# A four-layer token network on one core: norms by token, own waits, the ends, and the experts' down sums

## The chip, the core and the metric

The kernel runs on one core of a Trainium2 chip. The metric is device time in microseconds (us) of one execution; lower is better. A profiled execution gives a trace beside it. The engines are TensorE (PE, with its weight loads PEld), VectorE (DVE), ScalarE (ACT), GpSimd (POOL) and SyncE (SP, which issues most transfers).

## The reference

256 tokens of width 1024 pass a first block (two layers) and a second (two layers), all float32. The part that matters here:

```python
def _rmsnorm(x, g):
    xf = x.astype(jnp.float32)
    y = xf * lax.rsqrt(jnp.mean(xf * xf, axis=-1, keepdims=True) + EPS)
    return (y * g.astype(jnp.float32)).astype(x.dtype)
def adaln(x, g, shift, scale):
    return rmsnorm(x, g) * (1 + scale) + shift
# first block: x += mixer(rmsnorm(x)) @ w_out ; x += conv_ffn(rmsnorm(x)), twice
# second block, with a context of 256 more tokens in its first layer:
# x += mod * mixer(adaln(x)) @ w_out ; x += mod * (swiglu, then 8 experts)(adaln(x)); rmsnorm at the end
    for e in range(N_EXPERTS):
        ye = combine[:, e:e + 1] * swiglu(t, w1[e], w3[e], w2[e]).astype(jnp.float32)
```

The mixers are latent attention beside retention, gated linear attention, and window attention beside a matrix LSTM. Each token takes two of the eight experts.

## The kernel before

The residual `res` lies turned: the 1024 features are 8 tiles of 128 partitions, the 256 tokens (or 2 x 256 with the context) lie along the free axis. Each large product is made of three fast matmuls (`mm3`): a weight chunk is split into a rounded part (`weights_hi`, ScalarE, L1598) and a rest (`weights_lo`, VectorE, L2140), and so is the activation `h` (`h_rounded` on ScalarE, L1616; `h_rest` on GpSimd, L1384). Each engine runs its own program, written out by hand, and meets the others by semaphores. Weights come as 474 chunks, mostly of 1 MB, on SP's queue into a ring of 6 slots; three rounded chunks fit in `ring_hi`. `hi_upto` and `lo_upto` say how far the splits go before the next step of that engine.

There are nine norms with this layout, named in `NORM`: `even`, `ffn0`, `odd`, `ffn1`, `n1_0`, `n2_0`, `n1_1`, `n2_1`, `final`; `n1_0`, `n2_0` and `n1_1` take 512 tokens. In each, ScalarE squares two tiles at a time (`squares`, L1510), TensorE sums over the partitions with a 128x128 of ones, so that every partition gets each token's sum (`sum_squares`, L469; a column per token), ScalarE takes the root of all of it (`root`, L1536), VectorE the reciprocal and then the products with `res` and the gains (`norm`, L2110; L2124 in one instruction per tile, or L2120 for four tiles and L2122 per tile where there is a shift). `h` parts go on to ScalarE, GpSimd and TensorE tile by tile. `keep_warm` (L496) issues matmuls whose result nobody reads.

A `Lane` (L171) counts an engine's own instructions. `step` and `tell` wait for the instruction just issued before anything else is issued; `go` and `send` don't, and `settle` and `sent` wait later. `free` (L1464) marks a PSUM bank free, waits for it, and then raises a named flag; `leave` only marks the bank.

At the start SP loads the constants (with ones and eps among them), x, the columns and the rows of small parameters, then the chunks. VectorE computes the rotary angles, waits for ScalarE's sine, Silu, Exp and Ln, and works out the retention's decay rates in 16 small steps before it splits the chunks of the third projection.

An expert has 22 chunks for its up product and 11 for its down product (`down`, L1276): each of these held two rows of tiles by all 1024 columns, and both halves of 512 columns (PSUM banks 2 and 3) grew together. At the end of an expert ScalarE and VectorE take the two halves out (`expert_out`, L2045 and L2901), and `scatter` (L1217) adds the rows back to the tokens, during the next expert's up product. After the last expert that stands at the end: scatter, residual sums, norm `final`, four stores.

## Time and profile before

| | |
|---|---|
| median of 3 runs | 2541.44 us (2541.11 to 2541.6) |
| profiled execution | 2544.85 us |
| its span, first to last instruction | 2543.1 us |
| granted TensorE clock, mean | 0.97 of full |
| busy: PE, PEld | 2411.4 us (95%), 1996.7 us (79%) |
| busy: DVE, ACT, POOL | 1743.1 us (69%), 1243.2 us (49%), 523.2 us (21%) |
| moved from memory | 500.33 MB, 197 GB/s over the span |

The span is what the trace covers; 1.75 us of the profiled execution's time lie around it. Busy shares are means over stages with very different limits: what an edit is worth has to be read where it stands. The chain of waits is the chain of work that ended last, each step followed back to what released it; an entry there gives start, duration, engine and line. A releaser with a q behind its name is that engine's instruction queue. Matmul durations overlap each other, so a matmul's pitch is smaller than its duration.

### The profile page before, as it was taken

What the parts mean: (1) busy time and instruction counts of PE and PEld (TensorE: products, weight loads), DVE (VectorE), ACT (ScalarE), POOL (GpSimd) and SP (SyncE); (2) the same over time, 40 slices, a digit from 0 to 9 for tenths busy, and PEclk for the clock granted to TensorE, in tenths of its full rate; (3) what the DMA queues carried; (4) which work ended last, traced back from release to release, by engine and by line L of the source; (5) the groups of instructions that cost most, each with busy time, mean ns of one, the idle gap of its engine ahead of it and who ended that gap; (6) DMA issues with size and microseconds to landing.
All of it is one profiled execution on the core that took longest, in us unless ns stands there. A gap on an engine that the chain in (4) does not pass through costs nothing.

```text
span 2543.1 us, 35114 instructions
## 1 busy us (share of the span) xinstructions
PE 2411.4 (95%) x13296; PEld 1996.7 (79%) x13296; DVE 1743.1 (69%) x1895; ACT 1243.2 (49%) x1465; POOL 523.2 (21%) x407
## 2 busy tenths in 40 slices
PE   7999999999999999879999979979999999999997
PEld 5668998868997866658888867578888888888886
DVE  6556874567865766468645357657888888888886
ACT  5444444544433455332222134536777777777774
POOL 1003541004522000031003520003132132232231
PEclk9999999999999998889999989988999999999999
DMA  5574553414552310125555323026989989989894
GB/s 200 194 277 148 185 184 125 176 50 150 183 199 79 116 42 1 48 86 199 200 194 186 131 75 116 10 85 249 359 333 357 353 334 364 345 341 370 333 362 184
DMA packets 71461, 503.64 MB, mean 198 GB/s; under 512 B 8192, under 2 KB 8704, under 8 KB 11264
## 3 DMA queue, kind: packets, MB, share of 16 engines
q1 hardware_dynamic: 70128, 496.75, 53.4%
q0 software_dynamic: 1168, 4.66, 0.5%
q8 instruction: 107, 1.75, 0.3%
q14 instruction: 58, 0.48, 0.1%
HBM read 500.33 MB, written 1.05 MB: 197 GB/s over the span
## 4 chain that ended last, share of the span: by engine, by line
PE 86%; DVE 9%; ACT 3%; issue 1%; POOL 1%; DMA 0%; DVEq 0%; ACTq 0%; SPq 0%; PEldq 0%
PE ps L459 82%; DVE ring_r L2144 1%; PE ps L499 1%; DVE h L2122 1%; POOL h_r L1389 1%; DVE h L2120 1%; DVE areaA L2114 1%; PE ps L1214 1%; DVE h L2124 1%; PE ps L751 1%; DVE areaB L2638 1%; PE ps L602 0%; DVE temp L2207 0%; ACT ring_hi L1506 0%; ACT h L1553 0%
## 5 line engine op out<-in xcount | busy, mean ns | idle before, releaser
L1506 ACT ACTIVATE ring_hi<-ring 128x2048 fp32r<-128x2048 f32 x427 | 808.3, 1893 | 556.6 <-PE ps L459 333.3
L2898 DVE TENSOR_TENSOR ring_r<-ring,ring_hi 128x2048 fp32r<-128x2048 f32 x264 | 619.5, 2349 | 120.3 <-ACT ring_hi L1506 117.6
L459 PE MATMUL ps<-ring_hi,extra_r 128*128 128x512 f32 (+2 forms) x1808 | 612.2, 395 | 31.9 <-DVE ring_r L2144 18.1
L2144 DVE TENSOR_TENSOR ring_r<-ring,ring_hi 128x2048 fp32r<-128x2048 f32 (+3 forms) x163 | 384.3, 2358 | 190.9 <-ACT ring_hi L1506 176.4
L459 PE MATMUL ps<-extra_r,ring_hi 128*128 128x256 f32 (+1 forms) x1432 | 462.1, 323 | 22.3 <-POOL h_r L1389 20.8
L459 PE MATMUL ps<-extra_r,ring_r 128*128 128x256 f32 (+1 forms) x1432 | 457.1, 319 | 0.0
L459 PE MATMUL ps<-h_r,ring_hi 128*128 128x256 f32 (+2 forms) x1400 | 445.0, 318 | 0.0
L459 PEld LDWEIGHTS ps<-ring_hi,extra_r 128*128 128x128 f32 x1808 | 343.4, 190 | 107.1 <-DVE ring_r L2144 21.1
L459 PE MATMUL ps<-ring_r,extra_r 128*128 128x512 f32 (+2 forms) x1104 | 426.2, 386 | 0.0
L459 PEld LDWEIGHTS ps<-extra_r,ring_hi 128*128 128x128 f32 x1432 | 273.2, 191 | 46.5 <-POOL h_r L1389 24.1
L459 PEld LDWEIGHTS ps<-extra_r,ring_r 128*128 128x128 f32 x1432 | 273.2, 191 | 19.1
L459 PEld LDWEIGHTS ps<-h_r,ring_hi 128*128 128x128 f32 (+1 forms) x1400 | 267.2, 191 | 17.6
L459 PEld LDWEIGHTS ps<-ring_r,extra_r 128*128 128x128 f32 x1104 | 211.2, 191 | 38.7 <-issue 0.2
L1449 POOL TENSOR_TENSOR areaA_r<-areaA,cst 128x256 fp32r<-128x256 f32 x88 | 120.3, 1367 | 576.5 <-ACT areaA L2036 576.5
L459 PE MATMUL ps<-ring_hi,h_r 128*128 128x512 f32 (+2 forms) x400 | 150.3, 376 | 0.0
L1389 POOL TENSOR_TENSOR h_r<-h,extra_r 128x256 fp32r<-128x256 f32 x80 | 83.5, 1058 | 281.5 <-ACT extra_r L1506 281.4
L459 PE MATMUL ps<-ring_hi,areaB_r 128*128 128x512 f32 x352 | 139.8, 397 | 0.0
L459 PE MATMUL ps<-areaA_r,ring_hi 128*128 128x256 f32 (+1 forms) x736 | 139.5, 288 | 0.0
L459 PE MATMUL ps<-ring_r,areaA_r 128*128 128x512 f32 x352 | 138.0, 392 | 0.0
L459 PE MATMUL ps<-ring_hi,areaA_r 128*128 128x512 f32 x352 | 137.7, 391 | 0.0
L459 PEld LDWEIGHTS ps<-areaA_r,ring_hi 128*128 128x128 f32 x736 | 115.9, 192 | 1.3
L1409 POOL TENSOR_TENSOR areaA_r<-areaB,areaA_r 128x256 fp32r<-128x256 f32 x44 | 115.7, 2630 | 3.5
(356 smaller groups left out, 3123.2 us busy)
## 6 DMA issues: line engine op xcount, KB each, us to landing
ring<-in_experts SPq DMA_DIRECT2D x264, 1024.0 KB, 4.9
ring<-in_stream SPq DMA_DIRECT2D x202, 1024.0 KB, 4.9
ring<-in_stream SPq DMA_DIRECT2D x6, 512.0 KB, 3.6
ring<-in_stream SPq DMA_DIRECT2D x2, 576.0 KB, 3.6
res<-in_xT SPq DMA_DIRECT2D x1, 1024.0 KB, 5.7
res<-in_ctxT POOLq DMA_DIRECT2D x1, 1024.0 KB, 8.2
h<-in_consts POOLq DMA_DIRECT2D x2, 512.0 KB, 4.9
areaB<-in_cond_rows POOLq DMA_DIRECT2D x1, 1024.0 KB, 7.5
```

Of the source, the lines that this page charges most:

```text
L459: return pe.matmul(o, l, r, start=start, stop=stop, skip_group_check=True)
L499: pe.matmul(ps[:, u.bank, :], warm_l, warm_r, start=True, stop=True, skip_group_check=True)
L751: m = pe.transpose(ps[:, u.bank, k * P:(k + 1) * P], pair_p[:, 2 * (n % 2) + hd, k * P:(k + 1) * P], ident)
L1214: m = pe.transpose(ps[:, 3, s * P:(s + 1) * P], mprod[:, n % 2, s * P:(s + 1) * P], ident)
L1389: pool.tensor_tensor(h_lo[:, hf, k, :], h[:, hf, k, :], h_hi[:, hf, k, :].bitcast(F32), ALU.subtract).then_inc(sig("h_lo"), 1)
L1409: pool.tensor_tensor(lo, src, hi.bitcast(F32), ALU.subtract).then_inc(sig("hidden_ready"), 1)
L1449: pool.tensor_tensor(hi, mturn[:, n % 2, :], ones[:, 0:1].broadcast_to([P, NM]), ALU.mult).then_inc(sig("moe_hi"), 1)
L1506: return act.activation(dst, src, ACT.Copy)
L2114: S(dve.reciprocal(rs, rs))
L2120: S(TTN(h[:, hf, k:k + 4, :], res[:, hf, k:k + 4, :], bc(rs[:, hf * T:(hf + 1) * T], 1, [P, 4, T]), ALU.mult))
L2144: L.tell(TTN(ring_lo[:, s, 0:n], ring[:, s, 0:n], ring_hi[:, j % HIS, 0:n].bitcast(F32), ALU.subtract), "weights_lo")
L2898: TTN(ring_lo[:, s, :], ring[:, s, :], ring_hi[:, j % HIS, :].bitcast(F32), ALU.subtract).then_inc(sig("weights_lo"), 1)
```

## The change

It does five things. First, in eight of the nine norms (all but `even`) the sums are made with the squares as the stationary operand and one column of ones, so a token's sum stands on one partition: root and reciprocal work on 2 or 4 columns, and a new step `spread` on TensorE multiplies each column, read as a broadcast stationary operand, with the identity, so that every partition gets the values; VectorE's products read them from PSUM. Second, own waits become fewer on ScalarE and VectorE (`send`, `go`, `leave` in place of `tell`, `step`, `free`; about a third of them are shown), and `free` with a name raises the flag with the instruction itself. Third, the start: other load order, x in two loads, ones and eps by memset, 16 matmuls ahead, the splits of the first chunks between the products of `h`, and the decay rates (with ScalarE's Exp, Ln and Silu) moved behind the key heads. Fourth, the end: 9 matmuls, scatter by halves, 8 matmuls more, residual sums from the half that is ready. Fifth, the experts' down chunks hold four tiles of one half; the left half ends in the middle of the down product and is taken out while the right one grows. The residual adds and the merges are handled alike: a flag per second tile, and the next tile's scaling issued ahead of this tile's gate.

```diff
-    return up + [Piece("exp_w2_2", (0, x), c * 256, (c + 1) * 256, 0, D) for c in range(KF // 2)]
+    down = [Piece("exp_w2_2", (0, x), k * P, (k + 1) * P, a * 512, (a + 1) * 512) for a in range(2) for k in range(KF)]
+    return up + [down[4 * c:4 * c + 4] for c in range(KF // 2)]
...
-        ident, ones = keep("ident", P), keep("ones", P)
+        ident, ones, eps = keep("ident", P), sb("ones", [P, P])[:, :], sb("eps", [P, 1])[:, :]
+        rstd_tok = areaA[:, 10368:10372]
...
+                    last = hf not in [x[0] for x in steps[i + 1:]]
                     for kk in range(2):
-                        m = mm(ps[:, u.bank, hf * T:(hf + 1) * T], ones, temp[:, (2 * (i % 2) + kk) * T:(2 * (i % 2) + kk + 1) * T],
-                               i == 0 and kk == 0, kk == 1 and hf not in [x[0] for x in steps[i + 1:]])
+                        at = (2 * (i % 2) + kk) * T
+                        if tag == "even":
+                            m = mm(ps[:, u.bank, hf * T:(hf + 1) * T], ones, temp[:, at:at + T], i == 0 and kk == 0,
+                                   kk == 1 and last)
+                            continue
+                        for t in range(TT):
+                            c = TT * hf + t
+                            m = mm(ps[:, u.bank, c:c + 1], temp[:, at + t * P:at + (t + 1) * P], ones[:, 0:1],
+                                   i == 0 and kk == 0 and t == 0, kk == 1 and last)
                     if i < len(steps) - 1:
                         m.then_inc(sig("square_used"), 1)
                     else:
                         full(m, u)
+                        if tag != "even":
+                            spread(tag)
+
+            spreads = [0]
+
+            def spread(tag):
+
+                spreads[0] += 1
+                own = {"ffn0": 7, "odd": 7, "ffn1": 7, "n2_0": 6, "final": 0}
+                u = take("spread", tag, bank=own.get(tag, (turn[0] - 1) % 8))
+                keep_warm(u, 2)
+                pe.wait_ge(sig("rstd_tok"), spreads[0])
+                n = TT * len({hf for hf, _ in NORM[tag]})
+                for c in range(n):
+                    m = mm(ps[:, u.bank, c * P:(c + 1) * P], rstd_tok[:, c:c + 1].broadcast_to([P, P]), ident)
+                full(m, u)
 
             hs = (h_hi, h_lo)
             h_tiles = [0, 0]
...
+            for _ in range(16):
+                pe.matmul(ps[:, 7, 0:T], ones[:, 0:64].bitcast(BF16), ones[:, :].bitcast(BF16), start=True, stop=True,
+                          skip_group_check=True)
             sum_squares("even")
+            pe.wait_ge(sig("cst_loaded"), 16)
             first_split["even_in"] = len(splits)
...
-                        v = expert_weights(i, EXPERT_AT[e, KF + c], "p (k c) -> p k c", k=2)
-                        pe.wait_ge(sig("moe_hidden"), i * (NE * NP) + (e * NP + c + 3))
-                        steps = [(kk, a) for a in range(2) for kk in range(2)] if c == 0 else [
-                            (kk, a) for kk in range(2) for a in range(2)]
-                        for x, (kk, a) in enumerate(steps):
-                            kt = 2 * c + kk
-                            if c == 0 and x == 2:
-                                pe.wait_ge(sig("moe_turned"), i * (NE * NP) + (e * NP + NP + 1))
-                            m = mm3(ps[:, 2 + a, :], lambda s: hid[s][:, kt, :],
-                                    lambda s: v[s][:, kk, a * 512:(a + 1) * 512], kt == 0, kt == KF - 1)
+                        v = expert_weights(i, EXPERT_AT[e, KF + c], "p (k c) -> p k c", k=4)
+                        for x in range(4):
+                            a, kt = divmod(4 * c + x, KF)
+                            if a == 0 and kt % 2 == 0:
+                                pe.wait_ge(sig("moe_hidden"), i * (NE * NP) + (e * NP + kt // 2 + 3))
+                            m = mm3(ps[:, 2 + a, :], lambda s: hid[s][:, kt, :], lambda s: v[s][:, x, :],
+                                    kt == 0, kt == KF - 1)
                         m.then_inc(sig("moe_used"), 1)
...
-                            pe.wait_ge(sig("yexp"), i * (2 * NE) + (2 * e - 1))
+                            pe.wait_ge(sig("yexp"), i * (2 * NE) + 2 * e)
...
+                for _ in range(9):
+                    pe.matmul(ps[:, 0, :], warm_l, warm_r, start=True, stop=True, skip_group_check=True)
+                pe.wait_ge(sig("yexp"), i * (2 * NE) + 2 * NE - 1)
+                scatter(NE - 1, 0, 4).then_inc(sig("scattered_left"), 1)
                 pe.wait_ge(sig("yexp"), i * (2 * NE) + 2 * NE)
-                scatter(NE - 1).then_inc(sig("scattered"), 1)
-
-            pe.wait_ge(sig("scattered"), n_passes * 1)
-            for u in moe_acc:
-                pe.sem_inc(bank_full[u.bank], 1)
+                scatter(NE - 1, 4, 8).then_inc(sig("scattered"), 1)
+
+            for half in range(2):
+                pe.wait_ge(sig(("scattered_left", "scattered")[half]), n_passes * 1)
+                for u in moe_acc[2 * half:2 * half + 2]:
+                    pe.sem_inc(bank_full[u.bank], 1)
+            for _ in range(8):
+                pe.matmul(ps[:, 0, :], warm_l, warm_r, start=True, stop=True, skip_group_check=True)
             sum_squares("final")
...
-            sp.dma_start(cst[:, :], A["consts"][:, 0:NKEEP]).then_inc(sig("cst_loaded"), 16)
-            sp.dma_start(res[:, 0, :, :], A["xT"]).then_inc(sig("x_loaded"), 16)
-            sp.dma_start(cols[:, :], A["cols"]).then_inc(sig("const_loaded"), 16)
-            sp.dma_start(rows[:, :], A["rows"].partition_broadcast(P)).then_inc(sig("const_loaded"), 16)
+            for i in range(2):
+                sp.dma_start(res[:, 0, 4 * i:4 * i + 4, :], A["xT"][:, 4 * i:4 * i + 4, :]).then_inc(sig(f"x_loaded{i}"), 16)
...
+                if n == 0:
+                    sp.dma_start(cols[:, :], A["cols"]).then_inc(sig("cols_loaded"), 16)
+                if n == 1:
+                    sp.dma_start(cst[:, :], A["consts"][:, 0:NKEEP]).then_inc(sig("cst_loaded"), 16)
+                    sp.dma_start(rows[:, :], A["rows"].partition_broadcast(P)).then_inc(sig("rows_loaded"), 16)
...
-            ins.then_inc(bank_free[u.bank], 1)
-            lane.engine.wait_ge(bank_free[u.bank], u.nth + 1)
             if name:
-                lane.engine.sem_inc(sig(name), 1)
+                lane.tell(ins, name)
+                lane.engine.sem_inc(bank_free[u.bank], 1)
+            else:
+                ins.then_inc(bank_free[u.bank], 1)
+                lane.engine.wait_ge(bank_free[u.bank], u.nth + 1)
...
-                L.tell(copy(ring_hi[:, j % HIS, 0:size], ring[:, n % SLOTS, 0:size]), "weights_hi")
+                L.send(copy(ring_hi[:, j % HIS, 0:size], ring[:, n % SLOTS, 0:size]), "weights_hi")
...
-            squares("even")
             j = first_split["even_in"]
+            root("even")
             hi_upto(j + 1)
-            root("even", 4)
-            hi_upto(j + 2)
-            h_rounded(1)
+            h_rounded(1, {2: j + 2})
...
-            def norm(n, gain, shift=None, name="h_ready", split=False):
+            def norm(tag, n, gain, shift=None, name="h_ready", split=False, between={}):
                 norms[0] += 1
-                rs = rstds[:, 0:n * T]
                 L.wait("root_ready", norms[0])
-                S(dve.reciprocal(rs, rs))
+                if tag == "even":
+                    rs = rstds[:, 0:n * T]
+                    S(dve.reciprocal(rs, rs))
+                else:
+                    L.send(dve.reciprocal(rstd_tok[:, 0:n * TT], rstd_tok[:, 0:n * TT]), "rstd_tok")
+                    v = look(dve, "spread", tag)
...
+                        if i in between:
+                            lo_upto(between[i])
                         ins = STT(out=h[:, hf, k, :], in0=res[:, hf, k, :], scalar=gain(hf, k),
                                   in1=rs[:, hf * T:(hf + 1) * T], op0=ALU.mult, op1=ALU.mult)
                     if split:
-                        L.tell(ins, "h_raw")
+                        L.send(ins, "h_raw")
+                    elif k % 2 == 0:
+                        L.go(ins)
                     else:
-                        S(ins)
-                    if name == "out_ready" and k % 2:
-                        dve.sem_inc(sig(name), 1)
-                if name != "out_ready":
-                    dve.sem_inc(sig(name), 1)
+                        L.send(ins, name)
+                if tag != "even":
+                    L.sent("h_raw" if split else name)
...
-                S(TTN(t1, x1, s, ALU.mult))
-                S(TTN(t2, x2, s if s2 is None else s2, ALU.mult))
-                S(TTN(y1, x1, c, ALU.mult))
-                S(TTN(y2, x2, c if c2 is None else c2, ALU.mult))
-                S(TTN(y1, y1, t2, ALU.subtract))
+                L.go(TTN(t1, x1, s, ALU.mult))
+                L.go(TTN(t2, x2, s if s2 is None else s2, ALU.mult))
+                L.go(TTN(y1, x1, c, ALU.mult))
+                L.go(TTN(y2, x2, c if c2 is None else c2, ALU.mult))
+                L.settle(1)
+                L.go(TTN(y1, y1, t2, ALU.subtract))
+                L.settle(1)
...
-            lo_upto(j + 1)
-            norm(1, lambda hf, k: col("mix_even", k), split=True)
-            lo_upto(j + 2)
+            norm("even", 1, lambda hf, k: col("mix_even", k), split=True, between={2: j + 1, 4: j + 2})
...
+            L.wait("setup_act", 2)
+            u16, ln16 = stat[:, 80:96], temp[:, 256:272]
+            ser, small = temp[:, 272:288], temp[:, 288:304]
...
+                    if c == CPE - 3:
+                        dve.wait_ge(sig("wcur"), i * (2 * NE) + 2 * (e + 1))
+                        expert_out(i, e, 0)
+                    if c == 2 and e > 0:
                         expert_out(i, e - 1, 1)
```

The other hunks repeat these patterns: `L.tell` to `L.send` in `squares`, `h_rounded`, `pairs_hi`, `mixT_hi` and the Silu of the first block; `S` to `L.go` or `leave` in `pairs_lo`, the residual adds, `evacuate` and `ffn2`; on ScalarE the same move of `expert_out`, Sqrt loaded before the third projection's split, and the table functions moved behind the key heads' root.

## Rows read from the trace of the kernel before

**Rows 1.** The page's fourth part: shares of the chain that ended last.
```profile
PE 86%; DVE 9%; ACT 3%; issue 1%; POOL 1%; DMA 0%; DVEq 0%; ACTq 0%; SPq 0%; PEldq 0%
```

**Rows 2.** Windows: stretch, length, busy us per engine (count), PEclk, DMA share, GB/s.
```profile
38.00:44.00 6.00, 0.77 (x7) 0.61 (x6) 5.10 (x15) 5.49 (x6) 0.00 (x0) 0.73 0.49 173
426.50:429.70 3.20, 3.20 (x9) 2.51 (x9) 3.06 (x5) 1.49 (x4) 3.20 (x4) 0.50 0.00 0
...
2133.00:2232.00 99.00, 99.00 (x472) 82.04 (x471) 83.72 (x53) 71.10 (x59) 26.90 (x22) 1.00 0.92 349
```

**Rows 3.** Chain of waits before `ffn0`'s norm: start us, us, what.
```profile
219.03 1.15 PE ps L459 x4
...
220.26 0.48 ACT areaA L1540
...
220.81 1.76 DVE areaA L2114
...
223.62 8.73 POOL h_r L1389 x8
```

**Rows 4.** Chain of waits at norm `n1_0`, 512 tokens.
```profile
788.12 3.36 DVE areaA L2114
...
808.47 2.46 DVE ring_r L2144
```

**Rows 5.** Small operations: groups by line, one line each, and the chain.
```profile
L459 PE MATMUL ps<-stat,areaA_r 128*128 128x1 f32 x32 | 4.4, 241 | 0.0
...
L1544 ACT ACTIVATE stat<-stat,cst x14: 296/297/308, 50.0 to 1661.0; 128x4 f32<-128x4 f32 x8, 128x16 f32<-128x16 f32 x4, 128x2 f32<-128x2 f32 x2
...
L2362 DVE RECIPROCAL stat<-stat x1: 178/178/178, 50.7 to 50.7; 128x4 f32<-128x4 f32 x1
...
56.98 1.09 PE ps L839 x10
```

**Rows 6.** Chain of waits at norm `odd`: the second half of its first chunk.
```profile
433.77 5.75 PE ps L459 x24
```

**Rows 7.** Single lines: count, duration ns least/middle/most, first and last start.
```profile
L2124 DVE SCALAR_TENSOR_TENSOR h<-res,cols,areaA x40: 483/840/1040, 18.4 to 2540.0; 128x256 f32<-128x256 f32 x40
...
L1389 POOL TENSOR_TENSOR h_r<-h,extra_r x80: 718/881/2775, 19.5 to 1502.7; 128x256 fp32r<-128x256 f32 x80
...
L2501 DVE SCALAR_TENSOR_TENSOR areaB<-ps,cols,areaB x44: 482/482/486, 234.1 to 717.3; 128x255 f32<-128x255 f32 x44
...
L2120 DVE TENSOR_TENSOR h<-res,areaA x14: 1224/1628/1646, 791.5 to 1702.0; 128x1024 f32<-128x1024 f32 x14
...
L2122 DVE TENSOR_SCALAR h<-h,mods x56: 411/694/918, 792.8 to 1704.6; 128x256 f32<-128x256 f32 x56
```

**Rows 8.** Chain of waits at norm `n2_0`, its last parts.
```profile
1112.85 4.39 POOL h_r L1389 x3
```

**Rows 9.** Chain of waits in the first 60 us.
```profile
1.22 5.66 DMA res<-in_xT
...
18.43 0.50 DVE h L2124
...
35.75 1.28 ACT L1678
...
41.85 2.30 DVE ring_r L2144
...
44.20 12.78 PE ps L459 x48
```

**Rows 10.** VectorE in order of time near 107 us, with its idle time before.
```profile
107.66 0.75 DVE L2404 TENSOR_SCALAR areaB<-ps,cols 96x512 f32<-96x512 f32 x1 [7.02 <-PE ps L868]
```

**Rows 11.** Chain of waits behind the last expert's down sums.
```profile
2523.81 2.16 PE ps L459 x16
...
2528.02 5.62 PE ps L459 x16
...
2536.07 0.49 DVE h L2124
```

More of the change, by code:

```diff
@@ L135, in constants @@
     put("ident", np.eye(P))
-    put("ones", np.ones((P, P)))
     put("sel4", np.repeat(np.eye(4), P, axis=1))
@@ L143, in constants @@
     put("iota8", np.broadcast_to(8.0 - np.arange(8), (P, 8)))
-    put("eps", np.full((P, 1), EPS))
     inv16 = np.float32(10000.0) ** (-np.arange(16, dtype=np.float32) / np.float32(16))
@@ L1538, in root @@
                 squares(tag, a)
-                u, n = look(act, "norm", tag), T * len({hf for hf, _ in NORM[tag]})
-                free(L, act.activation(rstds[:, 0:n], ps[:, u.bank, 0:n], ACT.Sqrt, bias=eps, scale=1.0 / D), u,
+                u, n = look(act, "norm", tag), len({hf for hf, _ in NORM[tag]})
+                dst, n = (rstds, T * n) if tag == "even" else (rstd_tok, TT * n)
+                free(L, act.activation(dst[:, 0:n], ps[:, u.bank, 0:n], ACT.Sqrt, bias=eps, scale=1.0 / D), u,
                      "root_ready")
@@ L2017, in _ @@
                             L.wait("ffn_val", 2 * KF + m - 1)
-                        free(L, act.activation(fsil2[:, m % 2, :], ps[:, u.bank, :], ACT.Silu), u)
+                        leave(act.activation(fsil2[:, m % 2, :], ps[:, u.bank, :], ACT.Silu), u)
             for t in range(TT):
```

162 lines of the change are left out of this document (86 added, 76 removed).

## The prediction

> **What bounds the kernel now.** I read the page's fourth part first, then stages by window, then the chain of waits around each place that the change touches, then the rows of single lines. TensorE is 86% of the chain that ended last, VectorE 9%, about 229 us of 2543.1 [rows 1]. In the windows, from 2133 to 2232 us (one expert) TensorE is busy every microsecond at the full clock (2.4 GHz) [rows 2]. An edit there gains nothing unless it takes matmuls away, and this one takes none. So the time to be had lies where TensorE waits: the start, the nine norms, the end, and the chain of short steps in the mixers. From 38 to 44 us it works only 0.77 us of 6 [rows 2].
>
> **The norms, root and reciprocal per token.** Before, every norm holds the root of all tokens on all 128 partitions: one reciprocal of 128x256 takes 1.76 us [rows 3], of 128x512 3.36 [rows 4]. In the chain of ffn0 [rows 3] the last two sum matmuls (four instructions) start at 219.03, the root of 0.48 at 220.26, the reciprocal ends at 222.57, and the products follow: 3.6 us. After, for all but the first norm, four steps stand there. Sums: four matmuls with one column out, eight instructions. The nearest row has 128x1 matmuls at 4.4 us for 32 [rows 5], 0.14 each: 1.1, with the last one's end 1.3 (before 1.23 to the root's start). Root on 2 or 4 columns: 0.30, reciprocal 0.18 [rows 5]. Spread: a wait added on TensorE, then one matmul with the identity per 128 tokens, two instructions each. Ten instructions of identity transposes of 128x128 go in 1.09 [rows 5], 0.11 each: with the last one's end 0.6 for 256 tokens, 1.1 for 512. Handovers at 0.07 (from the root's end at 220.74 to 220.81 [rows 3]), 0.2 together.
>
> Sum for 256 tokens 2.6, saving 1.0; for 512 tokens the reciprocal's 3.36 becomes 0.18, the root loses 0.4, spread and its handovers cost 1.3, and the fillers (below) 0.3: saving 2.0, with roundings downward. What stands behind TensorE's new wait are ten filling matmuls (2.3 us at the 0.23 of a 512-column matmul: 24 in 5.75 [rows 6]) and the first weights of the next stage; they could not have started their real work earlier, since the first part of h comes 1.8 us after the first product. The two filling matmuls ahead of the wait cost 0.3 at the 512 norms (counted), where they start only once the sums' bank is free. Bounds per norm: 0 (spread twice as dear) and 1.5 (2.7 at 512). I take 1.0 and 2.0, by the rows.
>
> **The products and GpSimd.** The products read 1/root from PSUM now. Before, the row of L2124 shows 0.483 us at least, 0.84 in the middle [rows 7]: 0.48 alone, 0.85 while GpSimd subtracts (L1389, 0.718 at least, 0.881 in the middle). A product with one operand in PSUM (L2501) is 0.482 to 0.486 in all 44 cases [rows 7], though few of these lie beside GpSimd. I take 0.49 for the new product and 0.72 for GpSimd's. The 128x1024 products of the shifted norms go from 1.64 to 1.23 (L2120), their 128x256 scalings stay between 0.41 and 0.72 (L2122) [rows 7].
>
> The Trainium skill ("SBUF — State Buffer", Who interferes with whom) says that a VectorE instruction with two SBUF inputs contends with a GpSimd instruction that reads SBUF, and one with at most one SBUF input does not; L2124's two levels agree, and L2501's one level does too. It also says that a tensor_scalar in a two-port mode takes the pair, which the 0.41 and 0.72 of L2122 bear out. If the rule fails for this operand, the sum is that of rival A.
>
> What this gives GpSimd is partly taken back: the next weights' subtraction (2.3 us, both inputs in SBUF) now falls amid its parts, and GpSimd stands still for it.
>
> ffn0 and ffn1: GpSimd ends the chain (8.73 for 8) [rows 3]. From first product to last part of h 9.75 before; after 1.02 + 8 x 0.72 + 2.3 = 9.1. With the root's 1.0: 1.65 each, 3.3.
>
> odd: VectorE ends it. Eight products, 6.45, become 3.95; the same two fills; the subtraction starts 0.4 later beside GpSimd, and TensorE resumes not at 433.77 [rows 6] but near 430.4. TensorE's own first half (24 matmuls at 0.23 from 424.9) ends there too. 3.3.
>
> n1_0 and n1_1 (512): VectorE ends them, products 16.66 us, then the subtraction at 808.47 [rows 4]. Four 128x1024 products save 1.2, scalings that find GpSimd idle more often and need no own wait 1.1, less 0.3 for the subtraction's wait: 2.0 and 2.0 of the root make 4.0 each. n2_0: GpSimd's last three parts take 4.39 [rows 8] for the same reason; 16 x 0.73 + 2.3 against 17.7 leaves about 2 after VectorE's pace is allowed for, again 4.0. Together 12.
>
> n2_1 (no GpSimd beside it): 1.0 and own waits 0.2, 1.2.
>
> **The start.** x lands at 6.88, 5.66 after its issue, behind 0.49 MB of constants [rows 9]. The constants now go behind the second chunk of weights and x comes in halves; ones and eps are filled by VectorE. At the rate of that load the halves land near 4.4 and 5.7. After four squares and sums at 0.9 or 1.8 each the root starts near 8.9 if TensorE's clock is full (16 filling matmuls stand before them), 12.4 if it is at 1.2 GHz as before; the still wide root and reciprocal (0.48 and 1.76, as in [rows 3]) give first products at 11.3 or 14.9, against 18.43 [rows 9]. The weights' subtractions go between the products (after two and after four), ScalarE's second rounding between its h parts. By the rates above projection 0 ends 17.1 after the first product; before it ended at 33.3. Gain 4.9 or 1.3. Behind it, VectorE waited for ScalarE's Silu, Exp and Ln, each with a table load of 1.28 [rows 9], then took 16 small steps of its own, and only then came the subtraction at 41.85 for which TensorE waited until 44.20 [rows 9]. These all move to about 98 us; there VectorE idles 7.02 us until 107.66 [rows 10] and ScalarE waits for TensorE too, so they are hidden; without that cover the small steps would cost 3.3. The idle 5.2 us [rows 2] goes. SP issues three small loads later than the first chunks: the constants arrive by some 11.5, needed by the filling matmuls and then by VectorE's angles, in time. Late next is the latent scale before projection 3, 1 us ahead of its need. Gain 6.5 to 10.1; I take 8.3.
>
> **The end.** Before: the down sums end near 2521.6 (two steps of each half ahead of the scatter at 2523.81), scatter ends at 2525.97, then adds, sums in 5.62 us, much of it at 1.2 GHz, first product 2536.07 [rows 11]: 14.5 after the down sums. Now half the down sums leave during the second half. Nine filling matmuls (2.0 at 0.22) come first, scatter of the left half ends at 3.1, adds start at 3.3 instead of 4.5; squares, eight filling matmuls, four sums of 1.1, short root and spread: first product at 11.4. With products at 0.49 without own waits: 3.4. If the fillers fail to hold the clock, 2.
>
> **The rest.** Reordering the down sums costs nothing: the same 132 matmuls an expert, the same 1 MB chunks. The wait for a hidden pair comes every 1.4 us instead of 2.8; the last pair is due 13.8 us into the down sums, and GpSimd has it some 5 us in. Own waits and flags: the chain shows 0.03 to 0.07 at each (220.74 to 220.81 [rows 3] has a flag told after the instruction's own wait); some 60 on it change: 2.5 (bounds 0.5 and 5).
>
> Sum: 3.3 + 3.3 + 12 + 1.2 + 8.3 + 3.4 + 2.5 = 34.0. The profiled execution took 2544.85 (span 2543.1): 2510.85 after. The runs' median is 3.4 below it, so 2507.5.
>
> **Rivals.**
> A. PSUM doesn't free GpSimd: products stay at 0.85 and 1.64. For it: hardly one row of L2501 lies beside GpSimd. Against: L2124's low level with GpSimd still. Lost: 2.5 at odd, 0.65 twice, 1.5 three times, 1.5 at the start, 10 with the rest: 2517.5.
> B. Slower than before: the clock. The sums of 128x256 were work that kept TensorE occupied up to each norm; with one-column sums and a wait in the middle the next stage starts at 1.2 GHz. The window 426.5 to 429.7 stands at 0.50 [rows 2], 1.6 us lost. It decides once each of eight norms loses 4.3 us, some 8.5 us at half rate; at 4.8 the time is 2546. Against: in that window the clock came back after 3.2 us, with a longer pause ahead of it than there will be.
> C. The start doesn't keep its gain: ScalarE runs late (its rounding now waits among h parts, its Sqrt load stands before the latents) and TensorE waits at projection 2 or 3, and the 512 norms yield only the root: 5 and 6 lost, with 2 of small waits, 2520.
> D. More than forecast: TensorE never falls in clock and GpSimd gets ahead of the subtraction, 2498.
>
> **Chances.** Forecast 0.63 (2500 to 2515), A 0.13, B 0.05, C 0.14, D 0.05. The range is 2497 to 2523; it leaves out B and thin ends. Within 0.2% (5.1 us, what a measurement of this kernel tells from no change) I put 0.03, between B and C; slower 0.05; faster 0.92.
>
> **What would show it.** Reciprocals of 0.18 at eight norms and products of 0.49 with GpSimd near 0.72; subtractions amid GpSimd's parts, one part of about 2.8 in each norm. First projection at about 15 us, no idle stretch before the third. An expert's period unchanged at 99.4. The end 3 us shorter from the down sums to the last store. Wrong would be: products at 0.85, a granted clock of 0.5 for over 4 us after norms, or the experts' stage longer.

## The result and the profile after

The changed kernel takes 2504.78 us (median of 4 runs, 2503.26 to 2507.44), the kernel before 2541.52 in the same measurement: a ratio of 0.9851, 95% interval 0.9839 to 0.9863. In a later measurement it was 0.9848 (0.9829 to 0.9866), 2504.68 us. The forecast was 2507.5, with 2497 to 2523 as its range. The profiled execution took 2507.44 us, its span is 2505.6.

The page's fourth part, shares of the chain that ended last (the answer to [rows 1]):

```profile
PE 92%; DVE 4%; ACT 2%; issue 1%; POOL 0%; DMA 0%; DVEq 0%; ACTq 0%
PE ps L458 87%; PE ps L522 3%; PE ps L1241 1%; DVE h L2163 1%; DVE ring_r L2188 1%; PE ps L774 1%; DVE h L2161 0%; DVE temp L2253 0%; PE ps L625 0%; ACT h L1590 0%; ACT ring_hi L1542 0%; DVE h L2775 0%; ACT temp L2000 0%; POOL h_r L1422 0%; DVE h L2167 0%
```

VectorE fell from 9% to 4%. L522 is new near the top: these are the filling matmuls, now 3% of the chain (65.9 us over the pieces of the chain, against 33.9 before). They take longer than the work beside them: at several norms they run at half rate (3.4 to 4.3 us for ten, 2.2 at the full clock), and the products that they stand beside have become shorter. The windows (columns as in [rows 2]):

```profile
38.00:44.00 6.00, 6.00 (x29) 4.95 (x28) 0.50 (x5) 5.55 (x18) 0.00 (x0) 1.00 0.34 118
...
2100.00:2199.00 99.00, 99.00 (x472) 82.05 (x471) 83.50 (x53) 71.20 (x59) 21.65 (x22) 1.00 0.92 350
15.33:19.75 4.42, 4.42 (x11) 1.81 (x12) 4.42 (x4) 0.83 (x2) 4.42 (x4) 0.50 1.02 430
```

The idle stretch at 38 us is gone. An expert's stage is still full: TensorE is busy every microsecond of the 99, and ScalarE's first split of one expert follows that of the expert before by 99.39 us in both traces. The third stretch belongs to the start, below. Norm `ffn0` in order of time (start us, us, engine, line, what; the answer to [rows 3]), where L2153 is the reciprocal, L2167 the products, L1422 GpSimd's parts and L2188 the next weights' subtraction:

```profile
210.11 0.17 DVE L2153 RECIPROCAL areaA<-areaA 128x2 f32<-128x2 f32 x1 [2.10 <-ACT areaA L1577]
...
211.08 3.22 DVE L2167 SCALAR_TENSOR_TENSOR h<-res,cols,ps 128x256 f32<-128x256 f32 x8 [0.80 <-PE ps L458]
211.59 3.16 ACT L1542 ACTIVATE extra_r<-h 128x256 fp32r<-128x256 f32 x8 [1.51 <-DVE h L2167]
212.21 5.57 POOL L1422 TENSOR_TENSOR h_r<-h,extra_r 128x256 fp32r<-128x256 f32 x8
214.45 5.49 DVE L2188 TENSOR_TENSOR ring_r<-ring,ring_hi 128x2048 fp32r<-128x2048 f32 x1
```

Eight products take 3.22 us, one every 0.40, and GpSimd's eight parts go at 0.70 each beside them. But the subtraction, 2.3 us alone, lasts 5.49: it reads two operands from SBUF and ends only 2.2 us after GpSimd's last part. The forecast had it the other way round, with GpSimd standing still; so it came at the other five norms in which a spread feeds GpSimd (one part of 2.8 us each at odd, ffn1, n1_0, n2_0 and n1_1). Single lines of the whole run (answers to [rows 7]: duration ns least/middle/most):

```profile
L2167 DVE SCALAR_TENSOR_TENSOR h<-res,cols,ps x32: 471/472/483, 211.1 to 2502.7; 128x256 f32<-128x256 f32 x32
...
L2161 DVE TENSOR_TENSOR h<-res,ps x14: 1205/1208/1222, 774.9 to 1673.1; 128x1024 f32<-128x1024 f32 x14
...
L2163 DVE TENSOR_SCALAR h<-h,mods x56: 399/408/979, 776.1 to 1675.3; 128x256 f32<-128x256 f32 x56
...
L1422 POOL TENSOR_TENSOR h_r<-h,extra_r x80: 717/737/2826, 13.1 to 1477.7; 128x256 fp32r<-128x256 f32 x80
```

A product starts 0.40 us after the one before, though each lasts 0.47: they overlap. The products have one duration left, and so has the wide one; the middle of GpSimd's parts fell from 881 to 737 ns. The chain of waits at the start, the answer to [rows 9]:

```profile
0.77 3.69 DMA res<-in_xT
...
10.31 1.76 DVE areaA L2151
...
12.10 0.88 DVE h L2167 x2
12.99 2.21 DVE ring_r L2188
...
15.33 4.42 PE ps L522 x10
```

The first product starts at 12.10 instead of 18.43. Ten filling matmuls stand behind the wait for the weights' lower part and run at half rate (0.44 each, granted clock 0.50 in the third window above), so the first projection starts at 19.75, not at 15. The rows behind the last expert's down sums, which end at 2488.57 (answers to [rows 11]):

```profile
2488.57 1.96 PE ps L1345 x9
...
2494.60 3.51 PE ps L458 x32
...
2499.93 3.22 DVE h L2167 x8
```

Where the gain arises is read from the root of each norm (the time at which ScalarE starts it), in both traces:

| norm | even | ffn0 | odd | ffn1 | n1_0 | n2_0 | n1_1 | n2_1 | final |
|---|---|---|---|---|---|---|---|---|---|
| before, us | 14.4 | 220.3 | 421.4 | 581.1 | 787.4 | 1093.3 | 1481.4 | 1696.6 | 2533.7 |
| after | 9.7 | 209.8 | 408.5 | 565.7 | 772.2 | 1072.5 | 1457.6 | 1668.8 | 2498.1 |
| gained by then | 4.7 | 10.5 | 12.9 | 15.4 | 15.2 | 20.8 | 23.8 | 27.8 | 35.6 |
| same, second profile of after | 4.8 | 10.6 | 13.0 | 15.6 | 15.3 | 25.6 | 26.6 | 34.4 | 39.4 |

The two profiles of the same kernel agree within 0.2 us up to n1_0 and then differ by up to 6.6: behind some 940 us no single stretch of one profile tells an effect of under some 5 us.

### The profile page after: what moved, and what is told of

It is laid out like the page before. It is cut to its first block, busy times and chain, and to the rows that moved or that the text cites. A ratio compares the mean times of both kernels' runs of the same rounds, so it can differ in the third digit from the quotient of the medians.

```text
span 2505.6 us, 35253 instructions
## 1 busy us (share of the span) xinstructions
PE 2425.6 (97%) x13565; PEld 2015.4 (80%) x13565; DVE 1694.2 (68%) x1897; ACT 1223.1 (49%) x1463; POOL 476.4 (19%) x407
## 4 chain that ended last, share of the span: by engine, by line
PE 92%; DVE 4%; ACT 2%; issue 1%; POOL 0%; DMA 0%; DVEq 0%; ACTq 0%
PE ps L458 87%; PE ps L522 3%; PE ps L1241 1%; DVE h L2163 1%; DVE ring_r L2188 1%; PE ps L774 1%; DVE h L2161 0%; DVE temp L2253 0%; PE ps L625 0%; ACT h L1590 0%; ACT ring_hi L1542 0%; DVE h L2775 0%; ACT temp L2000 0%; POOL h_r L1422 0%; DVE h L2167 0%
## 5 line engine op out<-in xcount | busy, mean ns | idle before, releaser
L2188 DVE TENSOR_TENSOR ring_r<-ring,ring_hi 128x2048 fp32r<-128x2048 f32 (+3 forms) x163 | 384.9, 2368 | 183.3 <-ACT ring_hi L1542 169.3
L1482 POOL TENSOR_TENSOR areaA_r<-areaA,ones 128x256 fp32r<-128x256 f32 x88 | 110.6, 1257 | 607.7 <-ACT areaA L2074 607.7
L1422 POOL TENSOR_TENSOR h_r<-h,extra_r 128x256 fp32r<-128x256 f32 x80 | 73.5, 951 | 270.6 <-ACT extra_r L1542 270.5
```

Of the source, the lines that this page charges most:

```text
L1422: pool.tensor_tensor(h_lo[:, hf, k, :], h[:, hf, k, :], h_hi[:, hf, k, :].bitcast(F32), ALU.subtract).then_inc(sig("h_lo"), 1)
L1482: pool.tensor_tensor(hi, mturn[:, n % 2, :], ones[:, 0:1].broadcast_to([P, NM]), ALU.mult).then_inc(sig("moe_hi"), 1)
L2188: L.send(TTN(ring_lo[:, s, 0:n], ring[:, s, 0:n], ring_hi[:, j % HIS, 0:n].bitcast(F32), ALU.subtract), "weights_lo")
```

## The experiments

All start from the changed kernel. Ratios are to the kernel before, run beside them; the last column takes 0.985 off and multiplies by 2541.5 us (each with some 5 us of uncertainty either way, from the two intervals together).

| run | median, us | ratio (95%) | against changed |
|---|---|---|---|
| 1 norms as before | 2519.92 | 0.9906 (0.989 to 0.9923) | +14 |
| 2 start as before | 2514.12 | 0.9880 (0.9863 to 0.9896) | +8 |
| 3 end as before | 2508.23 | 0.9863 (0.9846 to 0.9879) | +3 |
| 4 own waits as before | 2518.28 | 0.9892 (0.9876 to 0.9909) | +11 |
| 5 spread copied to SBUF | 2522.61 | 0.9910 (0.9893 to 0.9927) | +15 |
| 6 four fillers | 2504.18 | 0.9851 (0.9831 to 0.9872) | 0 |
| 7 start's fillers early | 2504.72 | 0.9848 (0.9830 to 0.9867) | 0 |
| 8 changed, again | 2504.68 | 0.9848 (0.9829 to 0.9866) | 0 |
| 9 own waits in rotations | 2510.39 | 0.9864 (0.9846 to 0.9882) | +4 |
| 10 own waits in products | 2511.22 | 0.9875 (0.9858 to 0.9892) | +6 |
| 11 first norm spread too | 2506.29 | 0.9851 (0.9834 to 0.9869) | 0 |
| 12 6, 7 and 11 together | 2509.13 | 0.9857 (0.9834 to 0.9879) | +2 |

**1. The norms undone.**

```diff
-                if tag == "even":
+                if True:
                     rs = rstds[:, 0:n * T]
                     S(dve.reciprocal(rs, rs))
```

> The changed kernel with its norms alone undone: all nine take root and reciprocal over the full width in SBUF, as before, with no spreading matmuls; everything else stays changed. My forecast's sizes (ffn0, ffn1 1.65 each, odd 3.3, n1_0, n2_0, n1_1 4.0 each, n2_1 1.2) add to 19.8: 2504.8 + 19.8 = 2524.6 us. By the landmarks of the trace after (2.7 + 2.4 + 2.1 + 2.4 + 2.6 + 4.0 + 4.2, thinned waits within them included, end left out) 20.4: 2525.2 us, with ffn0 and ffn1 above and n1_0 and n2_0 below my sizes. Rival, that the spread is worth little since the fillers and the clock behind it take it back and the gain of those stretches is that of the thinned waits and the reordered ends: under 8 us, 2505 to 2513 us.

+14 us. At ffn0 the products start 2.3 us behind the root's start (in the changed kernel 1.3), and GpSimd's parts end the chain again:

```profile
209.76 1.76 DVE areaA L2151
...
212.57 7.97 POOL h_r L1422 x7
```

The norms are the largest part, though 6 us less than forecast. The rival's 8 us is out. Little of it lies in the first three: from ffn0's root to n1_0's this kernel takes 564.4 us and the changed one 562.4 in both of its profiles, 2.0 us for ffn0, odd and ffn1, where the forecast has 6.6.

What the short root and reciprocal save by themselves can be read from the end of the last square to the first product:

| norm | ffn0 | odd | ffn1 | n1_0 | n2_0 | n1_1 | n2_1 |
|---|---|---|---|---|---|---|---|
| run 1, us | 3.5 | 3.5 | 3.5 | 5.3 | 5.3 | 5.3 | 3.5 |
| changed | 2.4 | 2.9 | 2.9 | 4.3 | 4.3 | 5.9 | 2.9 |

Together 4.5 us; at n1_1 it is a loss, since the one-column sums run at half clock there (2.73 us from the last square to the root instead of 1.22).

**2. The start undone** (one load of x behind the constants, no first 16 matmuls, the decay steps with their table loads back at the front).

```diff
-            for i in range(2):
-                sp.dma_start(res[:, 0, 4 * i:4 * i + 4, :], A["xT"][:, 4 * i:4 * i + 4, :]).then_inc(sig(f"x_loaded{i}"), 16)
+            sp.dma_start(cst[:, :], A["consts"][:, 0:NKEEP]).then_inc(sig("cst_loaded"), 16)
+            sp.dma_start(res[:, 0, :, :], A["xT"]).then_inc(sig("x_loaded0"), 16)
...
```

> The changed kernel with the start alone undone: one load of the input behind that of the constants, no first 16 short matmuls, wide rounding steps in the old order, and the decay steps with their Silu, Exp and Ln back ahead of the first projections. My forecast's size of 8.3 us: 2513.1 us. By the first landmark of the two traces (58.07 to 48.19 us) 9.9 us: 2514.7 us. Rival, that the start is caught up with at the next wait for a weight or a transfer: under 3 us, under 2507.8 us.

+8 us. Its roots lie 8.9 to 11.2 us behind those of the changed kernel from ffn0 to n1_0 (218.7 against 209.8, 781.3 against 772.2), so what the start gains is kept that far; behind it the two profiles of the changed kernel differ too much to follow it, and the median has 8.

**3. The end undone.**

```diff
-    down = [Piece("exp_w2_2", (0, x), k * P, (k + 1) * P, a * 512, (a + 1) * 512) for a in range(2) for k in range(KF)]
+    return up + [Piece("exp_w2_2", (0, x), c * 256, (c + 1) * 256, 0, D) for c in range(KF // 2)]
...
-                for _ in range(9):
-                    pe.matmul(ps[:, 0, :], warm_l, warm_r, start=True, stop=True, skip_group_check=True)
```

> The changed kernel with the experts' down sums by pieces of 256 rows, both halves of an expert's result taken at its end, the last scatter in one and without the two groups of short matmuls behind it, as before. My forecast's size of 3.4 us: 2508.2 us. By the last landmark (the gain grows from 33.0 to 37.5 us behind the last expert) 4.5 us: 2509.3 us, with the expert period unchanged at 99.4 us. Rival, that the down sums by halves cost the experts what the end gains: 2503 to 2506 us.

+3 us, with an interval of the ratio that overlaps the changed kernel's: it fits 3.4 and 4.5 us and rules neither out nor in. An expert still takes 99.39 us, as in the two other kernels.

**4. All own waits back.**

```diff
-                L.go(TTN(t1, x1, s, ALU.mult))
+                S(TTN(t1, x1, s, ALU.mult))
...
-                        L.send(ins, "h_raw")
+                        L.tell(ins, "h_raw")
```

> The changed kernel with an engine's waits for its own last instruction put back at the places where the change thinned them. My forecast's size of 2.5 us: 2507.3 us. Rival, that nothing on the path that sets the end held such a wait, or that they only stood beside other work: within 0.5 us of 2504.8 us. Rival of the other side, that thinning is what the mixers gained (the landmarks show 27.4 to 27.5 and 20.1 to 22.4 us across them): 3 to 5 us, up to 2510 us.

+11 us, more than four times the forecast's 2.5 and over every theory that I had written down. The four runs lie in two pairs (2514.7 and 2515.2, 2521.4 and 2521.6), so 10 to 17 us above the changed kernel's median. The edit also puts back the order of the merges' steps, where the change had issued the next tile's scaling ahead. The timelines show what such a wait costs. Steps of a rotation on VectorE at the start of layer 1, in the changed kernel:

```profile
1526.76 0.42 DVE L2201 TENSOR_TENSOR temp<-areaA,cst 128x256 f32<-128x256 f32 x1
1527.10 0.42 DVE L2202 TENSOR_TENSOR temp<-areaA,cst 128x256 f32<-128x256 f32 x1
...
1528.90 0.22 DVE L2201 TENSOR_TENSOR temp<-areaA,cst 128x64 f32<-128x64 f32 x1
1529.04 0.22 DVE L2202 TENSOR_TENSOR temp<-areaA,cst 128x64 f32<-128x64 f32 x1
```

and with the waits back:

```profile
1535.93 0.43 DVE L2199 TENSOR_TENSOR temp<-areaA,cst 128x256 f32<-128x256 f32 x1 [0.15 <-DVE areaB L2681]
1536.39 0.42 DVE L2200 TENSOR_TENSOR temp<-areaA,cst 128x256 f32<-128x256 f32 x1
...
1538.69 0.22 DVE L2199 TENSOR_TENSOR temp<-areaA,cst 128x64 f32<-128x64 f32 x1
1538.95 0.22 DVE L2200 TENSOR_TENSOR temp<-areaA,cst 128x64 f32<-128x64 f32 x1
...
1540.51 2.29 DVE L2186 TENSOR_TENSOR ring_r<-ring,ring_hi 128x2048 fp32r<-128x2048 f32 x1
```

The reader is to subtract start from start: 0.34 without the wait and 0.46 with it, 0.14 and 0.26 for the small ones. The durations are alike. Without the wait an instruction starts before the one ahead of it has ended; the wait takes that overlap away, 0.12 us, and the chain shows only the 0.02 to 0.03 that are left between the two. The twelve steps last 4.3 us instead of 3.1. Behind them stands the subtraction for which TensorE waits in this kernel (the chain runs over VectorE from 1517.53 to 1542.86), while in the changed one TensorE goes on from 1510.98.

**5. The spread kept, its result copied to SBUF.**

```diff
-                    rs = ps[:, v.bank, 0:n * T]
+                    rs = rstds[:, 0:n * T]
+                    S(copy(rs, ps[:, v.bank, 0:n * T]))
```

> The changed kernel, but in the eight norms that spread by TensorE VectorE first copies the spread reciprocals from PSUM to SBUF, and its products read them there. Theory, that a product with an operand in PSUM leaves GpSimd's roundings alone and is itself left alone: products back from 0.40 to about 0.85 us apart where GpSimd works beside them, four 128x1024 products 1.2 us dearer in each of n1_0, n2_0 and n1_1, and the copies (0.45 us of 256 columns, 0.7 of 512): some 10 us above the changed kernel, 2515 us. Rival, that where the operand lies makes no difference: only the copies, 4.5 us, 2509 us, products at 0.40 us.

+15 us against 0.985, 17.9 against the changed kernel's median beside it: as slow as with the norms undone, although root and reciprocal are still done token by token. The timeline of ffn0, and the single line of the wide product:

```profile
212.14 5.66 DVE L2168 SCALAR_TENSOR_TENSOR h<-res,cols,areaA 128x256 f32<-128x256 f32 x8
...
213.16 8.66 POOL L1422 TENSOR_TENSOR h_r<-h,extra_r 128x256 fp32r<-128x256 f32 x8 [0.37 <-ACT extra_r L1542]
```

```profile
L2162 DVE TENSOR_TENSOR h<-res,areaA x14: 1218/1744/1759, 780.5 to 1688.1; 128x1024 f32<-128x1024 f32 x14
```

Eight products take 5.66 us instead of 3.22, GpSimd's parts 8.66 instead of 5.57, and the wide product 1.74 instead of 1.21. The copies put the first product 0.46 us later at the five norms of 256 tokens and 0.73 at the three of 512, 4.5 us together, as the theory had it; the other 10 or so are the operand's place. The rival (copies alone, 2509 us) is out.

**6. Four fillers in place of ten** behind each spread and ahead of the router.

```diff
-                    keep_warm(u, 10)
+                    keep_warm(u, 4)
```

> The changed kernel with 4 instead of 10 short matmuls behind each norm's spread and ahead of the router. They stand in the chain with 3.0 to 4.3 us for ten. Theory 1, that they are dead weight on the path: 1.5 to 2 us less at each of seven norms, 12 us less, 2493 us. Theory 2, that they are hidden beside the roundings: at ffn0 GpSimd's eighth part lands at 217.78 us and TensorE reads it at about 217.2 to 217.8 us, so TensorE would only wait later: within 2 us of the changed kernel, 2503 to 2507 us. Theory 3, that they bring the clock back: the first 20 or so matmuls run at 1.2 GHz, 0.12 us dearer each: 2 us more at each norm, 2518 us.

0 us (runs from 2498.9 to 2509.8). Theory 2 holds. At ffn0 real matmuls now start at 211.04 instead of 214.53 (where the first one's record starts; the chain puts the end of the fillers at 214.89), and TensorE then waits for the weights' subtraction, which GpSimd holds (chain of waits):

```profile
209.13 3.23 DVE h L2167 x8
...
212.50 5.54 DVE ring_r L2188
...
218.08 3.98 PE ps L458 x31
```

TensorE goes on at 218.08, when that subtraction has ended; and from this kernel's ffn0 root to its odd root it takes 198.3 us, in the changed one 198.7.

**7. The start's fillers ahead of the wait for the weights.**

```diff
+            for _ in range(10):
+                pe.matmul(ps[:, 7, 0:512], warm_l, warm_r, start=True, stop=True, skip_group_check=True)
+            warmed[0] = h_tiles[0] + 1
```

> The changed kernel with the ten short matmuls ahead of the first projection issued ahead of the wait for the weights' lower part, not behind it (they stood in the chain from 15.33 to 19.75 us). The first projection starts at 15.3 us instead of 19.75. Theory 1: GpSimd's parts five to eight land at 21.8 to 24.2 us, and TensorE waits for them in the second half of the first piece: 2 to 3 us less, 2502 us. Theory 2, that the idle stretch that is left between the fillers and the projection drops the clock: no gain, 2505 us. Theory 3, that all 4.4 us stay: 2500.4 us.

0 us. They start at 13.37, when the constants have landed, and the projection at 17.82, 1.9 us earlier than in the changed kernel, not 4.4. Of it 1.6 to 1.7 us are there at ffn0's root (208.1) and nothing in the median: with runs that spread by 4 us it can't be told from no gain.

**8. The changed kernel again.**

> The changed kernel as it stands, on the same chip as the three beside it. 2504.8 us, or 0.985 of the kernel before on that chip; it gives the three their baseline, and it shows how far two profiled executions of one kernel differ from norm to norm (0.5 us if the stretches repeat; some us if not).

As expected up to n1_0, not behind it (the table of roots above).

**9. Own waits back in the rotations alone.**

```diff
-                L.settle(1)
-                L.go(TTN(y1, y1, t2, ALU.subtract))
+                S(TTN(y1, y1, t2, ALU.subtract))
```

> The changed kernel with own waits put back in the rotary steps alone. Theory, from the timelines: an own wait behind a 128x256 product makes the next start 0.46 us after it instead of 0.34, behind one of 128x64 0.26 instead of 0.14, 0.12 us each, where the chain shows only 0.02 to 0.03 as issue; ten such waits stand in a layer's pair of rotations, and VectorE sets the end of the projections only at the start of layer 1: 1 to 3 us more than the changed kernel, 2506 to 2508 us, and the twelve steps at the start of layer 1 take 4.3 us instead of 3.1. Rival, that a wait costs the 0.03 us that the chain shows: 0.5 us, 2505 us, the twelve steps within 0.4 us of before.

+4 us by the ratio, inconclusive on the whole: its interval overlaps the changed kernel's, and one run took 2504.34. The starts are clear: 1528.83, 1529.29, 1529.75 for the products and 4.3 us for the twelve steps, as the theory had it.

**10. Own waits back behind the norms' products alone.**

```diff
-                        L.go(ins)
+                        S(ins)
```

> The changed kernel with own waits put back behind the products of the norms alone (some 150 instructions). Theory, that each costs 0.04 us where four 128x256 scalings went from 0.46 to 0.455 us each beside GpSimd, and 0.12 us where VectorE works alone: 0.2 us a group of five, 0.8 to 1 in each of n1_0, n2_0 and n1_1, less elsewhere, 3 to 4 us in all, 2508 us. Rival, that most of the 10 us that came back with all own waits lie here, since VectorE's products end these norms: 7 us or more, over 2511 us. Rival, that nothing is left of it: 2505 us.

+6 us, between the middle theory and the rival; its interval just touches the changed kernel's, so 1 us is possible as well as 11. One group (a wide product and four scalings) comes every 3.84 us against 3.50 to 3.55, and the twenty instructions of n2_0 take 15.35 us against 13.62: 1.7 in a norm of four groups, not 0.8. Eight products take 4.10 against 3.22. Runs 9 and 10 together come to 10 of the 11 of run 4, which the 5 us of uncertainty on each make no more than a fit.

**11. The first norm spread by TensorE too.**

```diff
+            sp.dma_start(cst[:, 0:P], A["consts"][:, 0:P]).then_inc(sig("ident_loaded"), 16)
...
-                if tag == "even":
-                    rs = rstds[:, 0:n * T]
-                    S(dve.reciprocal(rs, rs))
-                else:
+                if True:
```

> The changed kernel with its first norm done as the others: root and reciprocal token by token, spread by TensorE, products reading PSUM; the identity is loaded ahead of the first weights. Theory, that it is the operand in PSUM that pays: GpSimd's first four parts take 0.7 us each instead of 1.78, the reciprocal 0.2 instead of 1.76 us, and the first projection, whose ten short matmuls wait for the weights' lower part, starts 1.5 us earlier and waits for no part behind: 2 to 3 us less than the changed kernel, 2502 us. Rival, that the first weights (landing later behind the identity, and the subtraction that GpSimd holds) set the start: within 1 us, 2504 to 2505.5 us.

0 us; its first stretch is slower. The chain:

```profile
5.37 7.00 PE ps L458 x32
...
12.79 0.18 DVE areaA L2154
...
13.10 1.21 PE ps L458 x4
14.34 0.87 DVE h L2168 x2
```

Neither theory had this cost: one-column sums need 32 instructions instead of 16 and take 7.00 us, 0.22 each at the full clock where the rows had 0.14 [rows 5], not 4.45: the squares are now the weights, and loading them keeps TensorE's load side busy 6.90 of these 7.00 us. The reciprocal's 1.6 us are lost there, and the first product comes at 14.34 instead of 12.10. At ffn0's root it is 2.5 us behind the changed kernel (212.3 against 209.8), at n1_0's 1.6.

**12. Runs 6, 7 and 11 together**, with 16 short matmuls ahead of the first projection and the wait for the constants moved behind its first part.

```diff
-            pe.wait_ge(sig("cst_loaded"), 16)
+            for _ in range(16):
+                pe.matmul(ps[:, 6, 0:T], ones[:, 0:64].bitcast(BF16), ones[:, :].bitcast(BF16), start=True, stop=True,
+                          skip_group_check=True)
```

> The same first norm, with 16 short matmuls ahead of the first projection's waits instead of ten behind them, no wait for the constants ahead of it, and 4 instead of 10 short matmuls behind the other spreads and ahead of the router. If the parts add: 4 to 5 us at the start and 0 to 5 elsewhere, 2498 us. Rival, that what is won ahead of a stretch of full TensorE is given back in a lower clock, as the two kernels with such a change alone showed the median of the changed one: 2502 to 2505 us.

+2 us, no gain: no version beat the changed kernel.

## Why the prediction was right, and where its terms were not

The total came out 2.7 us from the forecast. The four undone parts add to 14 + 8 + 3 + 11 = 36 us, the whole is 38 (0.015 x 2541.5): as far as some 5 us of uncertainty on each can tell, they add up, and none hides another. The terms were less good than their sum: the norms came out 2 us or more below, the own waits 5 above, and that these cancel is luck.

**Norms: 19.8 forecast, 14 measured.** Up to 3.5 of the 19.8 were own waits of the products (1.1 in each of three norms, which also stood for scalings that find GpSimd idle, and 0.2 in n2_1), which run 1 keeps thinned and run 4 puts back. So 16.3 stand against 14, and 2.5 + 3.5 = 6.0 against 11. The kind of gain was right: products at 0.471 to 0.483 us in all 32 rows, GpSimd near 0.73, reciprocals at 0.17. The division was not. For root, reciprocal and spread the forecast had 1.0 at four norms and 2.0 at three, 10 us; the table under run 1 has 4.5, and run 5 leaves as much (14 less the 10 or so of the operand's place). The forecast priced sums, spread and the two fillers ahead of it at the full clock, and part of them runs at half of it at most norms (below). So the larger part of the gain is that the products read 1/root from PSUM, for which the forecast had some 6 without own waits. I had priced eight products at 3.95 us and they take 3.22, because they overlap.

The Trainium skill ("SBUF — State Buffer", Who interferes with whom) says that only a VectorE instruction with two SBUF inputs (or in a two-port mode) contends with GpSimd; runs 1, 5 and the changed kernel agree, 1.74 against 1.21 us for the same product. The same section adds that the order of issue decides who blocks. The subtraction at 214.45 was issued while one part of GpSimd was under way and did not come next: 5.49 us, with GpSimd's later parts unhindered. At odd, GpSimd's eight parts took 7.70 us beside two subtractions, so there it gave way. The rule names the port but not, in these rows, who gets it next.

**Where GpSimd does not give way.** "One part of about 2.8 in each norm" was wrong at ffn0 alone; at ffn1 the fourth part lasts 2.79 and the last ends 9.07 us after the first product, as forecast (9.1). At ffn0 it ended after 6.7 us; in its place the weights' lower part came late, 8.9 us after the first product. TensorE left its fillers at 214.89 either way, and did not meet that wait. With four fillers (run 6) it did.

**The clock: rival B's mechanism came true, its price did not.** One sign that I had named for being wrong, a granted clock of 0.5 for over 4 us after norms, did appear. These are the six microseconds from the root's start at ffn0 and n1_0, in the changed kernel:

```profile
209.80:215.80 6.00, 5.90 (x26) 3.08 (x25) 4.74 (x10) 4.47 (x10) 5.69 (x11) 0.72 0.58 236
772.20:778.20 6.00, 6.00 (x21) 3.20 (x19) 3.47 (x7) 3.46 (x6) 1.12 (x2) 0.54 0.09 33
```

and in run 1 (norms as before):

```profile
209.30:215.30 6.00, 4.15 (x23) 2.52 (x23) 5.50 (x7) 2.47 (x6) 4.69 (x9) 1.00 0.56 226
773.70:779.70 6.00, 2.09 (x10) 0.77 (x8) 5.24 (x5) 2.78 (x3) 0.00 (x0) 1.00 0.16 61
```

In this stretch the changed kernel has 0.50 to 0.73 at all eight norms (a mix of 1.2 and 2.4 GHz; in its second profile n2_1 keeps 1.00), run 1 has 0.90 to 1.00. TensorE works 5.65 to 6.00 of these 6 us at seven of the eight in the changed kernel, largely on fillers, and 2.1 to 4.3 in run 1. So the fall costs little: it is mostly fillers that run at half rate. As an estimate from the mean granted clocks (0.974 in all four runs of run 1, 0.969 to 0.972 in eight of the changed kernel) the spread takes some 5 to 12 us of full clock away over the whole run, much of it under waits. B needed 4.3 us at each of eight norms, 34 in all, to decide.

**ffn1 gave its gain back.** From ffn1's root to n1_0's the changed kernel takes 206.5 us, the one before 206.3, though TensorE works on 99.9% of it and before on 98.3. The windows behind the norm, the changed kernel and then run 7, whose ffn1 has the same instructions:

```profile
565.70:575.70 10.00, 9.90 (x47) 6.92 (x46) 5.70 (x10) 6.25 (x12) 6.80 (x7) 0.66 0.18 74
```

```profile
565.50:575.50 10.00, 8.52 (x60) 6.80 (x59) 6.11 (x10) 6.56 (x12) 7.61 (x8) 1.00 0.20 83
```

The granted clock is 0.66 over ten microseconds, with TensorE busy 9.90 of them and, at the full clock, 10.31 of the 10.70 us ahead. Runs 2, 4, 7, 10 and 11 keep the full clock there, wait for GpSimd's parts for 1.5 us of the window, and take 204.2 to 204.6 us for the stretch; runs 5, 6 and 9 fall like the changed kernel. So the low clock costs about 2 us here (206.5 against 204.4), and neither the spread nor the own waits decide it: runs 2, 7 and 11 differ from the changed kernel only at the start. What makes the clock fall in one and not in the other stays open.

**Start: 8.3 forecast, 8 by run 2, 9.9 by the traces.** The size fits, but by another division. First product at 12.10 was inside the forecast's 11.3 to 14.9. I had counted 17.1 us from there to the end of the first projection's first part and had not seen that its ten filling matmuls stand behind the wait for the weights (4.4 us): it ended 18.6 after, at 30.7. What made up for it lies behind: from there to the end of the transposes (48.19, before 58.07) the change gained 7.3 us where I had counted 5.2. The wait at 44.20 [rows 9] went altogether, and with it the low clock behind it (0.88 from there to 58.07; in the changed kernel 1.00).

**End: 3.4 forecast, 3 by run 3, 4.5 by the traces.** First product 11.4 us after the down sums, as forecast, and eight products 3.22 where they took 4.5.

**Own waits: 2.5 forecast, bounds 0.5 and 5; 11 with those of the products.** This is the term that failed. I read its price as the 0.03 to 0.07 that the chain shows between two instructions. The price is the difference of the pitches, 0.12 us, of which the chain shows a quarter. At 0.12 the 60 waits that I had counted come to 7.2, an estimate, and to 10.7 with the 3.5 of the products.

**Rivals.** A (PSUM does not free GpSimd) is refuted by L2167's row and by run 5, which shows what A describes: 2522.6, and 2518.1 without its 4.5 us of copies, against A's price of 2517.5. C is out: the start is kept up to n1_0 and in run 2's median. D's second half came true at ffn0 (GpSimd got ahead of the subtraction), without its gain; its first half, a clock that never falls, did not.

## What to carry to other kernels

Where VectorE's products and GpSimd slow each other down, move the small operand that the products read again and again into PSUM: here that is worth some 10 us of the change's 37, about twice what the shorter root and reciprocal gave. Price a wait of an engine for its own last instruction by start minus start with and without it, not by the gap that the chain of waits shows. A wait taken away uncovers the next one (here the held subtraction, then the fillers, then the clock), so undo parts one by one before crediting any of them.

## What the runs showed that I had not expected

- An own wait on VectorE costs 0.12 us on a product of 128x256 or 128x64 (from one start to the next 0.46 against 0.34, 0.26 against 0.14).
- With one-column sums and a spread the granted clock falls at the norm itself (0.50 to 0.73 in the six microseconds from the root, against 0.90 to 1.00 with wide sums), though TensorE is busy.
- A reciprocal of 128x256 in fp32 costs 1.76 us and one of 128x2 0.17.
- VectorE's subtraction of 128x2048 lasts 2.29 us alone and up to 5.5 beside GpSimd's back-to-back parts, which stay at 0.70.
- Executions of one kernel spread with the mean granted clock: run 12 took 2501.12 us at 0.972 and 2511.83 at 0.967, run 4 2514.7 at 0.970 and 2521.58 at 0.967.
